# Two transformer blocks on one core: the embedding product one expert later, the convolution's product inside the preceding group, the gates on column tiles, and no products whose result nobody reads

## The reference, cut to what matters

```python
# first block
z = rms_norm(x) @ w_in                       # pooling and 8 heads of attention on pieces of z
x = x + concat([y_pool, y_attn]) @ w_out
aff = softmax(h @ w_router)                  # 16 experts choose 32 tokens each
ye = (silu(xe @ w_gate[e]) * (xe @ w_up[e])) @ w_down[e]
x = x + scatter(ye * gates)
g = sigmoid(rms_norm(x) @ w_ple_gate)
e = rms_norm(p @ w_ple_proj)                 # the embedding product: needs nothing of x
x = x + g * e
# second block
h = rmsnorm(x)
gates = h @ w_in_2[:, 48 gate columns + 8 of i and f]
kv_c  = h @ w_in_2[:, 512 columns]           # then compressed by a small network
for g in range(4):                           # 4 groups of heads
    q, k (conv) = causal_conv(h @ w_in_2[...])   # 256 columns: the group's first product
    three kinds of NSA attention, one mLSTM head, one memory attention head
x = x + merge(...) @ w_out_2
x = x + ffn(x)
```

## Time and profile before

| | |
|---|---|
| three runs | 1737.37, 1737.71, 1734.03 us; median 1737.37 |
| profiled execution | 1731.99 us, of which the span of the trace is 1730.2 us |
| PE busy | 1363.9 us, 79%; in each of the first three of 40 equal slices 90% or more |
| DVE, ACT, POOL busy | 443.0, 187.5, 38.9 us |
| mean granted clock of PE | 0.914 |
| DMA | 517.75 MB, 299 GB/s over the span |

### The profile page before, as it was taken

How to read it: one execution, slowest core, us unless ns; L and a number is a source line. 1 busy time by engine, 2 the same in 40 slices (tenths; PEclk the granted TensorE clock), 3 DMA queues, 4 the chain that set the end, 5 groups by cost and what they waited for, 6 DMA issues and landing times.

```text
span 1730.2 us, 20248 instructions
## 1 busy us (share of the span) xinstructions
PE 1363.9 (79%) x8260; PEld 774.2 (45%) x8260; DVE 443.0 (26%) x951; ACT 187.5 (11%) x499; POOL 38.9 (2%) x104
## 2 busy tenths in 40 slices
PE   9997765666667666757666658999998999999997
PEld 5552211121212111211121113787777888599953
DVE  2432011011101110110011002333444001367775
ACT  2320100000000000000000001123434000100000
POOL 1100000000000000000000000000000000000000
PEclk9999879887878887987898889999999999999999
DMA  9668899999999999999999998112250336334342
GB/s 400 252 246 347 376 433 432 428 430 431 434 430 430 430 430 429 434 429 430 429 433 431 432 431 349 62 53 69 106 207 27 122 125 263 146 114 179 103 148 89
DMA packets 31040, 517.75 MB, mean 299 GB/s; under 512 B 3473, under 2 KB 4497, under 8 KB 6929
## 3 DMA queue, kind: packets, MB, share of 16 engines
q1 hardware_dynamic: 29072, 513.98, 71.0%
q10 hardware_dynamic: 1920, 3.11, 0.6%
HBM read 515.50 MB, written 1.05 MB: 299 GB/s over the span
## 4 chain that ended last, share of the span: by engine, by line
PE 51%; DMA 41%; DVE 5%; issue 2%; ACT 1%; SPq 0%; POOL 0%; ACTq 0%; PEldq 0%; DVEq 0%
PE ps L947 50%; DMA ring<-in_experts 40%; DMA scr<-in_w_ple_proj 1%; DVE turned_T L1592 1%; DVE scr L1705 1%; DVE xn L1829 1%; DVE scr L1818 0%; ACT xn L818 0%; DVE ps L1816 0%; DMA vecs<-in_vecs 0%; PE ps L953 0%; DVE ps L1815 0%; PE ps L1330 0%; PE ps L1037 0%; ACT scr L824 0%
## 5 line engine op out<-in xcount | busy, mean ns | idle before, releaser
L947 PE MATMUL ps<-ring,scr 128*32 128x512 f32 (+1 forms) x3066 | 482.1, 757 | 265.5 <-DMA ring<-in_experts 262.1
L947 PEld LDWEIGHTS ps<-ring,scr 128*32 128x32 f32 (+1 forms) x3066 | 122.1, 135 | 600.6 <-issue 310.9
L947 PE MATMUL ps<-turned_T,ring 128*128 128x128 f32 (+1 forms) x1952 | 321.2, 326 | 6.5 <-PE ps L947 2.6
L947 PEld LDWEIGHTS ps<-turned_T,ring 128*128 128x128 f32 x1952 | 291.6, 193 | 34.3 <-issue 8.9
L947 PE MATMUL ps<-scr 128*128 128x512 f32 (+9 forms) x668 | 138.9, 412 | 32.2 <-DVE scr L1705 13.0
L947 PE MATMUL ps<-ring,turned_T 128*128 128x128 f32 (+3 forms) x576 | 156.4, 430 | 2.0 <-DVE turned_T L1592 2.0
L947 PEld LDWEIGHTS ps<-ring,turned_T 128*128 128x128 f32 x576 | 94.3, 191 | 60.7 <-issue 46.6
L947 PEld LDWEIGHTS ps<-scr 64*128 64x128 f32 (+4 forms) x668 | 70.1, 174 | 97.0 <-issue 58.7
L1708 DVE TENSOR_TENSOR x<-x,ps 128x512 f32<-128x512 f32 x64 | 44.0, 687 | 214.0 <-PE ps L947 214.0
L1700 DVE SCALAR_TENSOR_TENSOR scr<-scr,ps 128x512 f32<-128x512 f32 x16 | 11.0, 687 | 271.4 <-PE ps L947 271.4
L1698 DVE SCALAR_TENSOR_TENSOR scr<-scr,ps 128x512 f32<-128x512 f32 x16 | 11.0, 687 | 239.2 <-ACT scr L739 239.2
(11 more groups left out here) (286 smaller groups left out, 868.0 us busy)
## 6 DMA issues: line engine op xcount, KB each, us to landing
ring<-in_experts SPq DMA_DIRECT2D x70, 4096.0 KB, 22.7
ring<-in_experts SPq DMA_DIRECT2D x48, 2048.0 KB, 20.7
ring<-in_w_ffn_in SPq DMA_DIRECT2D x11, 2048.0 KB, 7.8
ring<-in_w_merge SPq DMA_DIRECT2D x8, 1536.0 KB, 6.5
ring<-in_w_ffn_down SPq DMA_DIRECT2D x11, 1024.0 KB, 4.8
ring<-in_w_out SPq DMA_DIRECT2D x4, 2048.0 KB, 24.0
ring<-in_w_ml SPq DMA_DIRECT2D x4, 2048.0 KB, 7.8
ring<-in_w_nsa SPq DMA_DIRECT2D x4, 2048.0 KB, 7.7
```

Of the source, the lines that this page charges most:

```text
L947: return pe.matmul(o, l, rr, start=start, stop=stop)
```

## The change

1. PE goes from expert 0 straight to expert 1 and makes the aside after it; ACT and DVE do the same, and ACT's loads of the gain rows move too. SP keeps its order of loads; only its wait for `e_ps` before `w_mem_kv` moves behind expert 2's loads. 
2. The convolution product of group 0 is made before the wait for `em_sb`; those of groups 1 to 3 are made in the preceding group, one half before `values(n4, 0)` and one half before `values(n4, 1)`. They write the upper halves of banks 7 and 6, ACT copies them in two instructions instead of one, and the last group stands outside the loop.
3. The gates' weights (padded to 64 columns) become the stationary operand: 8 products with 256 moving columns, even and odd k on the two column halves of the array, once for both row tiles. ACT copies the two partial sums, and 2 + 2 small products with a constant matrix add them and turn them as needed.
4. The idle products go.

```diff
-PARTS = (1, 3, 3, 3, 3, 3)
+PARTS = (2, 2, 3, 3, 3, 3)
...
-            pe.wait_ge(idle_in, 1)
-            idle(6, sA[:, 0, 0, :])
             pe.wait_ge(in_ident, 32)
...
-            idle(5, ident)
             pe.wait_ge(route_sb, 3)
...
-            idle(22, ident)
             pe.wait_ge(route_sb, 4)
...
-            idle(4, ident)
             pe.wait_ge(sel_done, 2)
             pe.wait_ge(xn_done, 4)
             expert(0, FIRST_SLOTS, selall[:, 0], True)
+            expert(1, around(ROT), single=True)
             pe.wait_ge(in_mem, 48)
-            pe.wait_ge(x_acc, 4)
+            pe.wait_ge(x_acc, 8)
...
-                for k in range(KC):
-                    ins = mm(bank[4][:, t * 56:t * 56 + 56], hT[:, k, t * P:(t + 1) * P], wsm[:, k, :], k == 0, k == KC - 1)
-                    if t == 0 and k < 2:
-                        ins.then_inc(tfree[3 + k], 1)
                 if t == 0:
                     r.arrived(5, 1)
                 else:
+                    for k in range(KC):
+                        c = 64 * (k % 2)
+                        ins = mm(bank[4][c:c + 64, 0:T], wsm[:, k, :], hT[:, k, :], k < 2, k > 5)
                     ins.then_inc(ga_ps, 1)
...
                         for m in range(2):
-                            for u in range(NT):
-                                ins = pe.transpose(bank[5][0:4, m * T + u * P:m * T + (u + 1) * P],
-                                                   ifT[:, u, 4 * m:4 * m + 4], ident)
+                            ins = mm(bank[5][0:4, m * T:(m + 1) * T], const("both")[:, 48 + 4 * m:52 + 4 * m], gaT)
                         ins.then_inc(if_ps, 1)
+                        for u in range(NT):
+                            ins = mm(bank[4][:, T + u * 56:T + u * 56 + 56], gaT[:, u * P:(u + 1) * P], const("both"))
+                        ins.then_inc(ga_ps, 1)
...
+            def conv(m):
+
+                return product(bank[7 - m][:, T:2 * T], lambda k: tstrip[0][:, k, m * P:(m + 1) * P])
+
+            r.arrived(0, 1)
+            for m in range(2):
+                ins = conv(m)
+            ins.then_inc(proj_ps, 1)
+
             pe.wait_ge(em_sb, 1)
...
                 pe.wait_ge(ct_sb, g + 1)
+                pe.wait_ge(xt_sb, g + 1)
+                if more:
+                    r.arrived(0, 1)
+                    conv(0)
                 values(n4, 0)
...
+                if more:
+                    pe.wait_ge(ynsa_done, g * 2 + 1)
+                    pe.nop(nofuse=True)
+                    conv(1).then_inc(proj_ps, 1)
                 values(n4, 1)
```

More of the change, by code:

```diff
@@ L115, in constants @@
     put("fold", np.tile(np.eye(32)[:, 0:EXPERTS], (4, 1)))
+    put("both", np.tile(np.eye(64)[:, 0:56], (2, 1)))
     pool = np.zeros((len(POOL_WINDOWS), T, T), np.float32)
@@ L258, in two_blocks @@
         wr = small[:, 0:256].rearrange("p (k e) -> p k e", k=KC)
-        wsm = small[:, 256:704].rearrange("p (k e) -> p k e", k=KC)
-        w2 = small[:, 704:832]
+        wsm = small[:, 256:768].rearrange("p (k e) -> p k e", k=KC)
+        w2 = small[:, 768:896]
         sq = sb("sq", 24 + 2 + 8)
@@ L381, in two_blocks @@
         gth = E2(NT * 48, "p (t n) -> p t n", t=NT)
[L382 removed]
+        gaT = E2(T)
         iR, fR, mnR, abR, lnR, BR, aR, MR, mR, emR, nMR = (E2(T, parts=4) for _ in range(11))
@@ L517, in with_aside @@
             def with_aside(part, quarter):
+                paired(sum(PARTS[:part]), around(ROT))
                 if quarter:
-                    paired(sum(PARTS[:part]), around(ROT))
                     sp.wait_ge(mkv_ps, quarter)
                 else:
[L523 to L527, removed]
                     sp.wait_ge(e_ps, 4)
@@ L532, in _ @@
             expert(0, FIRST_SLOTS, FIRST_LOADS)
+            for n, s in enumerate(around(ROT)):
+                if n == 4:
+                    sp.wait_ge(h_sb, 1)
+                    sp.dma_start(*whole(9, "w_ple_proj", 0)).then_inc(full[9], 16)
+                r.load(s, strip_of(s, 1, n))
             for n in range(4):
@@ L750, in _ @@
             expert(0)
+            expert(1)
             for c, n in enumerate(("norm_ple_post", "g_post_mix_2", "g_post_ffn_2")):
@@ L795, in _ @@
             act.wait_ge(ga_ps, 1)
-            gates = bank[4][:, 0:2 * 56].rearrange("p (t n) -> p t n", t=NT)
-            act.activation(ifT, gates[:, :, 48:56], ACT.Copy).then_inc(ga_th, 1)
+            act.activation(gaT, bank[4][:, 0:T], ACT.Copy).then_inc(ga_th, 1)
+            act.wait_ge(ga_ps, 2)
+            gates = bank[4][:, T:T + 2 * 56].rearrange("p (t n) -> p t n", t=NT)
             act.activation(gth, gates[:, :, 0:48], ACT.Tanh, scale=0.5).then_inc(ga_th, 1)
@@ L1193, in experts @@
             def experts(part, rot):
[L1194 to L1198, removed]
+                with pe.Fori(0, PARTS[part]) as i:
                     r.enter(i, PAIRED)
-                    expert(i + sum(PARTS[:part]) + first, around(rot))
-                    r.leave(PARTS[part] - first)
-            idle(4, ident)
+                    expert(i + sum(PARTS[:part]), around(rot))
+                    r.leave(PARTS[part])
             pe.wait_ge(sel_done, 2)
@@ L1272, in _ @@
                         ins = mm(o, tstrip[5][:, k, g * P:(g + 1) * P], hT[:, k, t * P:(t + 1) * P], k == 0, k == KC - 1)
+                        if t == 0 and g == 0 and k < 2:
+                            ins.then_inc(tfree[3 + k], 1)
                     if t == 1 and g % 2:
@@ L1344, in _, with group @@
             memq = tslot[1][:, 0:D].rearrange("p (k n) -> p k n", k=KC)
-            with pe.Fori(0, GROUPS) as g:
-                r.enter(g, {0: (1, 1), 1: (1, 1), 5: (1, 1)})
+            def group(g, more):
                 n4 = g * 4
-                r.arrived(0, 1)
-                for m in range(2):
-                    ins = product(bank[5][:, m * T:(m + 1) * T], lambda k: tstrip[0][:, k, m * P:(m + 1) * P])
-                ins.then_inc(proj_ps, 1)
                 r.arrived(5, 1)
@@ L1443, in _ @@
                 pe.wait_ge(ymem_done, g + 1)
-                r.leave(GROUPS)
+            with pe.Fori(0, GROUPS - 1) as i:
+                r.enter(i, {0: (1, 1), 1: (1, 1), 5: (1, 1)})
+                group(i, True)
+                r.leave(GROUPS - 1)
+            group(GROUPS - 1, False)
             pe.wait_ge(ynsa_done, 8)
```

26 lines of the change are left out of this document (10 added, 16 removed).

## The result

| | before | changed |
|---|---|---|
| runs beside each other | 1734.03 to 1737.71 us (4), median 1735.86 | 1714.56 to 1719.31 us (4), median 1718.12 |
| ratio, 95% interval | | 0.9894, 0.9874 to 0.9915 |
| profiled execution, its span | 1731.99, 1730.2 us | 1717.3, 1715.5 us |
| mean granted clock of PE | 0.914 | 0.908 |

The change is faster by 1.1%, 17.7 us between the medians. The two profiled executions differ by 14.7 us only.

A forecast was written before the change was run, and what follows sets the result against it. DMA was taken to bound the experts from 191.20 to 1057 us, PE the stages behind them. The terms summed to -11.0 us: 1721.0 for an execution like the profiled one, 1726.4 as a median, range 1718 to 1733.

The forecast's parts named there:

- aside after expert 1: Experts: the DMA hole from 185.50 to 191.20 us goes, -4.4 us, bounds 0 and -4.4.
- no idle products: Start and routing: PE falls to half clock without them, +2.0 and +2.7 us.
- gates: Mixer's entry: fewer gate products and a half-clock stretch that ends earlier, -2.1 us, bounds +0.1 and -4.
- conv of group 0: Ahead of group 0: the moved product fills a 1.66 us wait at full clock, -2.9 us, bounds -1.0 and -3.8.
- conv inside the group: Three group borders: product halves fill PE's idle, 2.1 us each, -6.3 us, bounds 0 and -9.7.
- b: Experts: the DMA hole comes back behind expert 1, 1730.8 us; chance 0.11.
- c: Group borders: the moved halves fill nothing and each border stays as long, 1732.7 us; chance 0.12.
- d: Attention pairs: clock stays at 0.50 without the first six products, so slower; 50 us would give 1751; chance 0.07.
- (a): Start and routing: the half clock costs nothing, falling on work that waits anyway, 1721.7 us; chance 0.14.
- the offset: Whole kernel: the runs' median is 5.4 us above the profiled execution, carried over to the changed kernel.
- The start: First turns and what follows: half clock without the six idle products, +2.0 us, bounds 0 and 3.3.
- the routing's +2.7: PE's path from 132.41 us to slot 0 runs at half clock, +2.7 us, bounds 0 and 2.7.

The follow-up runs named there:

- control: The kernel before, unchanged, run once more for a second profile (also written e1): 1737.11 us, ratio 1.0006.
- e4: The kernel before with only the aside moved behind expert 1: 1729.85 us, ratio 0.9959.
- e5: The kernel before with only the new gates: 1731.19 us, ratio 0.9974.
- e6: The kernel before with only the moves of the convolution products: 1726.48 us, ratio 0.9930.
- e8: The kernel before with the first row tile's small gate products behind its kvc products, nothing removed: 1734.5 us, ratio 0.9992.
- e7: The changed kernel with the convolution products of groups 1 to 3 back at the heads of their groups: 1730.07 us, ratio 0.9958.
- e10: The changed kernel with only the six idle products at the start back: 1714.31 us, ratio 0.9891.
- e14: The changed kernel with the six idle products at the start back and eleven short fillers at the mixer's entry: 1713.16 us, ratio 0.9866.
- e15: The changed kernel with only the six idle products at the start back, run a second time: 1713.37 us, ratio 0.9865.
- e2: The kernel before with only the idle products taken out: 1739.94 us, ratio 1.0012.
- e9: The changed kernel, unchanged, run once more: 1718.65 us, ratio 0.9894.
- e13: The changed kernel with all idle products back, plus 4, 4 and 3 more in the mixer entry's three waits: 1713.18 us, ratio 0.9860.
- e3: The changed kernel with all idle products back at their four places: 1715.68 us, ratio 0.9878.
- e11: The changed kernel with only the routing's 31 idle products back: 1723.69 us, ratio 0.9928.
- e12: The changed kernel with all idle products back, plus 14, 14 and 10 more in the mixer entry's three waits: 1718.54 us, ratio 0.9903.

## Why the prediction was right in direction and wrong in size

By its own steps, each read at PE's milestones against the control, or against the kernel before where that is the same:

| step | predicted | measured | where |
|---|---|---|---|
| aside after expert 1 | -4.4 | -5.9 | last load of e4; its time -7.1 (4.5 to 9.5) |
| no idle products | +4.7 | +3.4 in the profile, 1.3 to 5.7 in four | slot 0's load |
| gates | -2.1 | -3.8 | changed kernel and e5; time of e5 -4.5 |
| conv of group 0 | -2.9 | -4.0 | changed kernel and e6 |
| conv inside the group | -6.3 | -6.7 | periods of 50.08 for 52.32 |
| sum | -11.0 | -17.0 | |

The first group's scores come 1155.16 - 1144.67 = 10.5 us earlier than in the control, the FFN 15.0 earlier; of the -17.0 the half clock in the last group gave 2.4 back (the profile's -14.7). No rival took place: no second hole (against b), the halves filled the borders (against c), the attention did not stay at half clock (against d: at most 3.5 us late at its end), and (a), that the clock costs nothing, is refuted by the rows above though its time, 1721.7, was nearer.

Two steps failed: the sizing of four terms, and the offset that was carried from the profiled execution to the median. Of the 6.7 us between the forecast of 11.0 and the 17.7 between the medians, 3.7 lie in the profiled executions (the table's 6.0 less the 2.4 of the last group) and 3.0 in the offset. In the four terms the mechanism was right, and each came out better by 1.1 to 1.7 us:

1. *Aside.* The term was the busy share of one window laid by hand around the hole. Its edges cost too; 5.9 lies outside the bounds given, and 0.9 of it no window here places.
2. *Gates.* "If it ends 3.3 earlier, 1.6 is won; I take half, -0.8". The stretch does not end earlier, it goes as a whole, 3.1 us: of the 5.05 that the first row tile lost (12.30 from gates to turn before, 7.25 now), 2.0 are the products and the rest is clock; e8 shows this clock without removing any product. Against it the second row tile's gates and small products cost +1.3 (13.61 us from its turn to the compression for 12.35), not +0.7. The column halves did run side by side: 1.95 us where one after another 3.5 was worked out. The drain between tiling modes of which the Trainium skill warns ("TensorEngine Tiling (Array Packing)", Key Properties) does not show beside the wait of 0.94 for DVE that was there before.
3. *Group 0.* "I take 1.8 down to 1.0" for fear that the small products behind let the clock fall. They don't: 1.00 from 1118 to 1131.
4. *Idle products.* The start was taken at +2.0 in one piece. It is 1.0 or 3.5, by execution, and their mean over five profiles, 2.5, is nearly the forecast; the routing's +2.7 arises nearly in full only in some executions (in the changed kernel's first profile 2.3 of the 3.4 lie there, in e7 0.2), and with the start at full clock it is 0.2 to 1.2 (e10, e14, e15), no more than kernels with all idle products lose there too.

The groups' borders were right: 2.1 forecast from the rows laid out anew, 2.24 measured.

The offset: "the median of the runs is 5.4 higher, and I carry the difference over to it". The changed kernel's median is only 0.8 above its profiled execution (1718.12 and 1717.3). That the medians differ by 17.7 and the profiles by 14.7 lies with the kernel before: both of its profiled executions (1731.99, and the control's span of 1730.5 with 1.8 around it) lie 4 to 5 us below its medians, the changed kernel's first lies 1.3 below its own (1718.65 over nine runs). What the slower executions of before lose has no profile here and stays open; stretches of half clock that come and go, as those in e2 and e4 inside the group loop, are the candidate.

The removal of the six products at the start was a loss inside the gain: the changed kernel with them back runs at 1713.8 us in the median of eight runs (e10, e15), 4.9 below the changed kernel's 1718.65, and slot 0 comes 3.4 earlier (138.8 for 142.2, the means of the table's rows). (Beside each other e10 and e9 have ratios of 0.9891 and 0.9894 with wide intervals; e15's 0.9865 is the clearer one.) That form, e13 and e14 (1713.2 each) are the fastest found, 1.1 to 1.4% below before, and not told apart.

## What to carry to other kernels

Where PE sets the time, price the granted clock as its own term: read which stretches are at 0.50, what stands on them, and move the thin products (here 56 moving columns) behind the thick ones or give them wide moving operands; order alone was worth 3.3 us in one profile here, though the times do not confirm it. A gain that rests on several uncertain parts should not be cut at each of them: four terms taken on the cautious side added up to 5.6 us of 17. Idle products paid at the start (some 4 us), where PE sets the pace of what follows; in the routing their worth did not stand out once the start ran at full clock. When you add some, count them in records, since each float32 one is two.

## What the runs showed of the hardware

- A stretch of half clock belongs to an execution as much as to a kernel. Two profiles of the changed kernel: kvc at 7.41 and at 9.04 us, start 1.0 and 3.5 us late, a stretch in the last group in one only. Read in windows of 1 us behind the experts, the stretches with a granted clock under 0.99 were

```
before, e1   1090-1098  1125-1132            changed  1320-1328
e2           1097-1105  1131-1139            e9       1090-1095
             1186-1190  1240-1248            e10      1085-1089
e4           1084-1092  1118-1126 1279-1287  e15      none
e5           1123-1131  1178-1182            e3       1107-1122
e8           1121-1129                       e7       1109-1124  1280-1287
e6           1092-1100  1328-1339            e11      1111-1126  1326-1337
e12, e14     1322-1327, 1316-1321            e13      1318-1329
```

(without the last stretch of each, at the end of the kernel). The Trainium skill ("TensorE: Matmul & The Clock Gate", Part 1) says that the monitor behind the clock runs free of the kernel's start, so that the moment of a change moves from run to run. The two profiles of the changed kernel fit that; they do not show the cause.
- The longest of these, on compression products that kept PE busy for all of 13.8 us in e3, cost 5.7 us: 12.16 for 8.60 and 9.27 for 7.17. PE was fully occupied there and the clock did not rise for 13.8 us.
- Idle products of 128x128 took 0.117 us a record in a filled wait (28 records in 3.29 us, e12).
- Eight products of 64 stationary and 256 moving columns, even and odd ones on the two column halves, took 1.95 us; eight of 128 stationary and 256 moving columns took 3.71.
